# Input squares two per unit, accumulator sums two units later, and products without a use in the gaps of three transitions, in a one-core encoder trunk

## What is computed

```python
for i in range(DEPTH):
    mod = cond @ ada_w[i] + ada_b[i]
    sh_t, sc_t, g_t, sh_c, sc_c, g_c = jnp.split(mod, 6, axis=-1)
    h = modulate(rms_norm(x, norm_g[i, 0]), sh_t, sc_t)
    h = s5_mixer(h, ...) if i % N_MIXERS == 0 else diff_attention(h, positions, ...)
    x = x + g_t[:, None, :] * rms_norm(h, norm_g[i, 1])
    h = modulate(rms_norm(x, norm_g[i, 2]), sh_c, sc_c)
    h = conv_ffn(h, ffn_w_in[i], ffn_conv_w[i], ffn_conv_b[i], ffn_w_out[i])
    x = x + g_c[:, None, :] * rms_norm(h, norm_g[i, 3])
```

## Time and profile before

| | us |
|---|---|
| median of 3 executions | 1444.52 |
| lowest and highest | 1440.93, 1446.57 |
| the profiled execution, its own time | 1442.14 |
| its span, first to last instruction | 1440.3 |
| TensorE busy in the span | 1279.6 (89%) |
| VectorE busy | 828.2 (58%) |
| ScalarE busy | 510.2 (35%) |
| GpSimd busy | 411.2 (29%) |
| mean granted clock of TensorE, of full speed | 0.917 |

### The profile page before, as it was taken

The page is one execution under the profiler, slowest core; times in us unless marked ns, Lnnn a source line. Parts: engine busy times, 40 slices in busy tenths (PEclk is TensorE's granted clock), DMA queues, the critical chain, the costliest instruction groups (busy, mean ns, idle before and its releaser), DMA issues.

```text
span 1440.3 us, 17450 instructions
## 1 busy us (share of the span) xinstructions
PE 1279.6 (89%) x6330; PEld 1003.3 (70%) x6330; DVE 828.2 (58%) x1131; ACT 510.2 (35%) x777; POOL 411.2 (29%) x264
## 2 busy tenths in 40 slices
PE   3674599879969899999889999989889999999995
PEld 0244588658857788888768767656668888888884
DVE  8979857776846354324584466664674444443223
ACT  2054244324413243313331334443534433432211
POOL 3991000025545234300021332420024343341001
PEclk9586799979979899999989999997889999999997
DMA  8562955414653222323213212211103223223221
GB/s 347 216 234 39 162 201 212 175 59 161 235 188 122 82 88 87 117 96 109 99 59 117 73 45 73 58 44 59 59 30 117 87 88 116 87 87 117 96 80 58
DMA packets 35431, 164.99 MB, mean 115 GB/s; under 512 B 4528, under 2 KB 14000, under 8 KB 17200
## 3 DMA queue, kind: packets, MB, share of 16 engines
q1 hardware_dynamic: 34368, 163.97, 33.8%
q10 hardware_dynamic: 1008, 0.27, 0.1%
HBM read 156.95 MB, written 3.08 MB: 111 GB/s over the span
## 4 chain that ended last, share of the span: by engine, by line
PE 76%; DVE 13%; DMA 4%; issue 3%; ACT 2%; SPq 1%; DVEq 0%; ACTq 0%; POOL 0%; POOLq 0%
PE psum L1723 16%; PE psum L1724 15%; PE psum L1725 15%; PE psum L1833 5%; PE psum L1834 5%; PE psum L1835 5%; PE psum L1888 3%; DMA ada_raw<-in_ada_w 2%; PE psum L1891 1%; PE psum L1912 1%; SPq L372 1%; PE psum L1579 1%; DVE ada_acc L1239 1%; PE psum L1873 1%; PE psum L1875 1%
## 5 line engine op out<-in xcount | busy, mean ns | idle before, releaser
L1723 PE MATMUL psum<-hhi,whi 128*128 128x512 f32 x960 | 385.5, 402 | 7.8 <-DVE hlo L1315 6.9
L1724 PE MATMUL psum<-hlo,whi 128*128 128x512 f32 x960 | 378.7, 394 | 0.0
L1725 PE MATMUL psum<-hhi,wlo 128*128 128x512 f32 x960 | 378.4, 394 | 0.0
L1176 DVE TENSOR_TENSOR wlo<-raw,whi 128x2048 fp32r<-128x2048 f32 x81 | 191.4, 2362 | 179.3 <-ACT whi L680 179.3
L551 POOL TENSOR_TENSOR ca<-ca,cb 128x512 f32<-128x512 f32 x44 | 148.6, 3378 | 269.9 <-ACT ca L789 269.9
L1723 PEld LDWEIGHTS psum<-hhi,whi 128*128 128x128 f32 x960 | 183.7, 191 | 50.6 <-issue 10.2
L680 ACT ACTIVATE whi<-raw 128x2048 fp32r<-128x2048 f32 x80 | 153.2, 1914 | 166.9 <-PE psum L1835 146.1
L1725 PEld LDWEIGHTS psum<-hhi,wlo 128*128 128x128 f32 x960 | 183.2, 191 | 38.9
L1724 PEld LDWEIGHTS psum<-hlo,whi 128*128 128x128 f32 x960 | 183.9, 192 | 36.7
L1343 DVE SCALAR_TENSOR_TENSOR ca<-psum,convp,ca 128x511 f32<-128x511 f32 x44 | 33.0, 749 | 247.7 <-ACT ca L785 247.7
L1833 PE MATMUL psum<-ghi,whi 128*128 128x512 f32 x352 | 137.2, 390 | 1.5 <-DVE wlo L1176 1.5
(11 more groups left out here) (339 smaller groups left out, 1811.5 us busy)
## 6 DMA issues: line engine op xcount, KB each, us to landing
raw<-in_units SPq DMA_DIRECT2D x92, 1024.0 KB, 4.8
ada_raw<-in_ada_w SPq DMA_DIRECT2D x24, 1024.0 KB, 5.0
ada_ring<-in_ada_w SPq DMA_DIRECT2D x24, 1024.0 KB, 4.8
toep<-toeplitz_rows SPq DMA_DIRECT2D x32, 128.0 KB, 7.6
qk_sw<-ca SPq DMA_DIRECT2D x32, 128.0 KB, 2.3
u<-in_x_blocks SPq DMA_DIRECT2D x1, 2048.0 KB, 14.0
x<-in_x_t SPq DMA_DIRECT2D x1, 2048.0 KB, 8.4
out_t<-x SPq DMA_DIRECT2D x8, 256.0 KB, 2.0
```

Source lines behind the costliest of these rows:

```text
L1176: TT(wlo[:, s, :], raw[:, s, :], whi[:, s, :].bitcast(F32), ALU.subtract).then_inc(split_lo, 1)
L1723: M(out, w_hi, hi[:, k, :], start=(k == 0), stop=False)
L1724: M(out, w_hi, lo[:, k, :], start=False, stop=False)
L1725: return M(out, w_lo, hi[:, k, :], start=False, stop=(k == KT - 1))
```

## The change

Three edits.

In the units of the gated linear unit, ScalarE squares tiles 2i and 2i + 1 of x in unit i for i < 4, and none in units 4 to 7; VectorE adds them in the same units, in the same place of its order.

`reduce_acc` of the second and of the third sum stands before MLP units 10 and 14 in place of 8 and 12. The second waits for 19 steps in place of 20 (the last step of slot 1 is number 18).

In `barrier(r)` for r = 0, 1, 2, TensorE makes 31 products of 128 x 512 whose result nobody reads: 7 into bank 7 ahead of the wait for `ssum` (behind a wait for a weight split that was counted before), 6 into bank 3 behind the small sums, 6 behind the first row product, 12 behind the second.

```diff
--- before.py
+++ after.py
@@ -726,9 +726,9 @@
                 A(ca[:, s, :], psum[:, 2 * s + 1, :], ACT.Sigmoid).then_inc(sig_ready, 1)
                 if i < N_GLU - 1:
                     split_high(i + 2, s, i // 2 + 1)
-                    if i == 0:
-                        x_square(0)
-                    x_square(i + 1)
+                if i < KT // 2:
+                    x_square(2 * i)
+                    x_square(2 * i + 1)
                 if i == 0:
                     act.wait_ge(mod_read, 1)
                 glu_squares(i)
@@ -1397,7 +1397,10 @@
                 TT(y_glu[:, i, :], psum[:, 2 * s, :], ca[:, s, :], ALU.mult).then_inc(y_ready, 1)
                 if i < N_GLU - 1:
                     split_low(i + 2, s, None)
-                    x_square_add(i + 1)
+                    if i < KT // 2:
+                        if i:
+                            x_square_add(2 * i)
+                        x_square_add(2 * i + 1)
                     ada_step(i, s, i // 2 + 1, i, 0)
                 tile_sums(0, i)
 
@@ -1764,8 +1767,16 @@
                     ins.then_inc(glu_half, 1)
             ins.then_inc(unit_done, 1)
 
+            def idle_products(n, bank):
+
+                for _ in range(n):
+                    M(psum[:, bank, :], whi[:, 0, 0:P], whi[:, 0, 0:SEQ], start=True, stop=True)
+
             def barrier(r):
 
+                if r < 3:
+                    pe.wait_ge(split_lo, (U_FIN[0], U_V, U_FIN[1])[r] + 1)
+                    idle_products(7, 7)
                 pe.wait_ge(sum_a, 7 * r + 7)
                 for t in range(QT):
                     ins = M(psum[:, 4, t:t + 1], ssum[:, P * t:P * t + P], col[:, 0:1], start=True, stop=True)
@@ -1779,13 +1790,16 @@
                         ins = M(psum[:, 6, QT + t:QT + t + 1], cb[:, 1, P * t:P * t + P], col[:, 0:1],
                                 start=True, stop=True)
                     ins.then_inc(stat_c, 1)
+                    idle_products(6, 3)
                 pe.wait_ge(spread1, r + 1)
                 M(psum[:, 5, :], ones[:], diag[:].rearrange("p t s -> p (t s)"), start=True,
                   stop=True).then_inc(row1_psum, 1)
                 if r < 3:
+                    idle_products(6, 3)
                     pe.wait_ge(spread2, r + 1)
                     M(psum[:, 7, :], ones[:], on[:].rearrange("p t s -> p (t s)"), start=True,
                       stop=True).then_inc(row2_psum, 1)
+                    idle_products(12, 3)
 
             def ffn(layer):
                 n0, g0 = U_FIN[layer], layer * JT
@@ -1808,11 +1822,11 @@
                     ins = gemm_step(1, KT + k, hhi, hlo)
                 ins.then_inc(unit_done, 1)
                 if layer == 0:
-                    for third, (lo, hi, slot) in enumerate(((2, 8, 0), (8, 12, 1), (12, 14, 0))):
-                        pe.wait_ge(ada_added, KT * (third + 1) + 4 * (third == 1))
+                    for third, (lo, hi, slot) in enumerate(((2, 10, 0), (10, 14, 1), (14, 16, 0))):
+                        pe.wait_ge(ada_added, (KT, 2 * KT + 3, 3 * KT)[third])
                         reduce_acc(slot, THIRD * (3 + third))
                         pairs(pe, lo, hi, body)
-                    pairs(pe, 14, JT, body)
+                    pairs(pe, 16, JT, body)
                     pe.wait_ge(mod_ready, 1)
                 else:
                     pairs(pe, 2, JT, body)
```

## The result

The changed kernel takes 1405.33 us (median of 4 executions, 1403.8 to 1406.4) against 1444.47 for the kernel before on the same chip (4 executions, 1440.93 to 1446.57): a ratio of 0.9731, with a 95% interval from 0.9708 to 0.9753. The profiled execution of after took 1404.48 us (span 1402.7), that of before 1442.14 (span 1440.3).

A forecast was written before the change was run, and what follows sets the result against it. TensorE's stalls, plus half the 1.2 GHz time after them, were taken as the bound. Gains 7.4 + 26.9 + 5.0 = 39.3 us took the profiled 1442.1 to 1402.8; 2.4 more for the median gave 1405, range 1397 to 1415.

The forecast's parts named there:

- Part 1: Between units 6 and 7: idle wait and slow clock go, 7.8 us, less 0.4 for VectorE's queue: 7.4 us gained.
- Part 2: Sums before units 8 and 12, moved to 10 and 14, cost 5.2 us each: gain 16.7 + 10.2 = 26.9 us.
- rival B: Units 8 and 9: VectorE's two steps per unit become the bound, giving back 6 to 9 us; 1411 to 1414, chance 0.10.
- Part 3: Three transitions: useless products, hidden in gaps, bring the clock back; 5 us gained, bounds -6.5 to +6.
- (a): Stages behind the three transitions start at 2.4 GHz: 1.6 + 1.4 + 1.4 = 4.4 us gained.
- (b): Second row product in each transition takes about 1.0 us less, VectorE waits only 0.24 us for it: 0.7 us gained.
- (c): First transition: small sums ran slow and VectorE waited 0.62 us for them; up to 0.4 us gained.
- such a dip makes groups two and three late by some tenths of a us: In most transitions the clock falls, then rises during groups two to four; the stage-start gain stays whole.
- if a group's end sets the start of a row product: In the transitions: one of the signs named beforehand that would show the forecast wrong; no size given.
- Rival A: Transitions: clock stays at 1.2 GHz, useless products bring nothing or cost 0 to 6.5 us; 1410 to 1417, chance 0.15.
- Rival C: Transitions: useless products lie on TensorE's path, costing 40.0 us if all are slow and uncovered; 1450, chance 0.02.
- Rival D: At the three waits something else is as late, so only part 3 stays; 1439 to 1446, chance 0.03.

The follow-up runs named there:

- squares alone: The kernel before with only the two input squares per unit added: 1438.05 us, ratio 0.995.
- sums alone: The kernel before with only the second and third accumulator sums moved before units 10 and 14: 1419.04 us, ratio 0.9811.
- products alone: The kernel before with only the 31 useless products in each of three transitions added: 1440.62 us, ratio 0.9972.
- 7, 0, 0, 12: The changed kernel without the second and third groups of useless products in each transition: 1405.99 us, ratio 0.9715.

## Why the prediction was right, and where it was not

**Part 1, forecast 7.4, measured 7.9** in the pair of traces (19.77 to 11.83), and 7.2 by time in squares alone. Both steps held: the small products took 0.95 us at full speed, and the stretch behind them has no slow product. The gap of transition 0 grew as forecast by VectorE's queue: it is 18.31 and 18.32 us in the two kernels with the old squares and no products, 18.70 and 18.68 in the two with the new squares and no products, 0.4 us. Net of that, 7.5.

**Part 2, forecast 26.9, measured 25.6** (260.73 to 235.14), and 27.3 by time in sums alone. The rows give the account term by term. The three sums cost 4.25 + 19.03 + 13.46 us before from large product to large product, and 4.25 + 3.72 + 3.72 after. The slow large products behind them, from the starts of the next thirty or so at 0.227 us each, cost 1.60 + 2.99 + 2.16 before and 2.80 + 1.71 + 1.70 after. Together 43.5 and 17.9: a difference of 25.6, the whole of what was measured. A sum cost 3.72 - 0.23 + 1.70 = 5.2 us, the price that the prediction read from the first one. That both did so in this execution is partly luck: nine traces have 17 such sums in front of units 10 and 14, in one block and without a wait, and 11 of them cost 5.2 us and 6 cost 6.8 (the third sum of the changed kernel's second execution among them: 4.05 - 0.23 + 2.99). What the prediction missed is the sum that isn't moved: its slow products cost 1.2 us more than in before (the clock was down for 6.83 us and not 3.41 as in the earlier trace rows). The other kernels have from 1.5 to 3.0 us there, sums alone 1.7, so this is scatter and not a price of part 2.

**The counts and VectorE (rival B) fell as forecast.** There is no wait of TensorE between units 8 and 10; VectorE's two steps per unit fit.

**Part 3, forecast 5, measured 3.5** in the pair of traces (0.7 + 1.2 + 1.2, and the 0.4 that part 1 costs in transition 0), 4.0 by time in products alone (0.0019 of the time either way, so 1.3 to 6.8), 2.8 as the difference of the medians' ratios with and without. Against the mean of the four traces without products (166.6) the two of after (161.5 and 161.4) gain 5.1, but the spread of those four, 164.6 to 169.0, is nearly as large as the effect. The size is therefore known to some 2 us and no better. By terms: (a), forecast 1.6 + 1.4 + 1.4, is 1.3 + 1.1 + 1.1 by the stages alone (23.18 to 21.86, 66.81 to 65.73, 23.91 to 22.79). That is 3.5 of 4.4: the stages start at 2.4 GHz, but the first product and some that wait for VectorE's tiles still start late, and 96 products take 21.86 us where they take 21.53 in the kernel with 7, 0, 0, 12. (b) and (c), forecast 0.7 and up to 0.4 in shorter gaps, did not come: the gaps changed by +0.6 (0.4 of it part 1's), -0.1 and -0.1.

The step that was wrong for the gaps is "such a dip makes groups two and three late by some tenths of a us". The dip came where it was put, and in transition 0 it lasted 6.8 us and made the two row products 1.4 and 1.6 us later behind the last large product (9.72 to 11.13, 12.80 to 14.42, of which 0.4 are VectorE's lateness of part 1). Since the stage follows the second row product's end by 3.4 us, the 1.25 us left of the second ate the 1.05 that this product gained by running in 1.02 us in place of 2.07: 0.2 us lost where (b) and (c) had up to 0.6 gained. The prediction had named this as a sign of being wrong ("if a group's end sets the start of a row product"), and it holds at both row products of transitions 0 and 2 and at the second of transition 1. In transitions 1 and 2 the row products were later by 0 and 0.5, and by 0.6 and 0.2 us, and that cost nothing there. But (b) came to 0.1 us each, because of something else that VectorE waits for: it no longer waits for the second row product, but for a tile of x from GpSimd. In transition 1, before and now:

```profile
724.29 0.76 DVE L1327 SCALAR_TENSOR_TENSOR psum<-x,pre_a,psum 128x512 f32<-128x512 f32 x1 [0.25 <-PE psum L1787]
...
691.57 0.76 DVE L1327 SCALAR_TENSOR_TENSOR psum<-x,pre_a,psum 128x512 f32<-128x512 f32 x1 [0.16 <-POOL x L544]
```

The floor of part 3's range is off by a little too: -1.9 twice and -2.5 make -6.3, not -6.5.

**Rival A** (the products bring nothing) had the mechanism half right: the second and third group bring nothing, as the kernel with 7, 0, 0, 12 shows. It was wrong on the fourth, which makes the stage start fast whatever the clock did before it. **Rival C** fell, but its mechanism is there: by 67 products per transition in place of 31 the transitions cost 19.4 us more. **Rival D** fell: the waits went, and the stretches shortened by what they had cost.

**Was the total right by chance?** In part. Against the same pair of traces the forecast terms were 0.1 low, 1.3 high and 1.5 high; 1.2 us of untouched attention and a start of -0.4 came on top. The sum missed by 39.3 - 37.6 = 1.7 us, and the median by 0.3. That the median is so near is luck: errors of 1 to 2 us partly cancelled, and one more slow third sum would have added 1.6. The terms are what was tested.

**What stays open.** Why the clock is down for 3.41 us at the first sum in one kernel and 6.83 in another, and why a like sum costs 5.2 us in one execution and 6.8 in the next. That it varies was seen, in two executions of one kernel too; what sets it was not tried. The transitions of the kernels without products were each seen in one trace only.

## What to carry to other kernels

Ask of each stall what it costs altogether: its wait, the small work behind it at half speed, and the large products until the clock is back; here 6.2 us of waiting made a sum cost 15.4 us (13.46 - 0.23 + 2.16) that mostly costs 5.2 without it, and at times 6.8. A consumer that only needs its input some time later is best moved behind the point at which the producer is surely done, and first into a wait that exists anyway, where it costs nothing. Filler products pay right in front of the stage that needs the clock, as many as end just before its input is ready; in the middle of a gap they delayed what stands behind them here by as much as they sped it up, and once by 1.3 us more.

## What the runs showed of the hardware beyond what was expected

- Small f32 products of one column do not hide among large ones: 0.22 us each in a block (3.5 us for 16) and 0.24 between large products (0.92 against 0.68 us per step). The Trainium skill, "TensorE: Matmul & The Clock Gate", section "Wait — 56ns, not 53.3ns?", has about 25 ns as the least from start to start of a small product. By it the 32 rows of a sum would take at least 0.8 us (an estimate: 32 x 25 ns); the trace has 3.62, far above that least.
- TensorE that is busy with small products alone is granted less all the same: behind 3.62 us of them, without a wait, the large products behind the second sum started every 0.43 us from the sixth on, and behind the third from the second on (clock rows of the result: means 0.63 and 0.53). In the kernel with four large products (1.17 us) in the midst of a transition's small ones it was at 0.50 before the last of these ended.
- One small product ahead of every three large ones, for a whole unit (14.68 us), left the clock at 1.00.
- In the kernel with 7, 0, 0, 12 the second row product ran at half speed, the twelve large products behind it took 4.96 us, and the stage after them ran at 0.23 us per product from its first row on.
